# A pair of column blocks by seven products, and a plan laid a second time from its end

## What is computed

```python
h = rms_norm(x, norm_g) @ w_in
c_q, c_kv, k_pe, qkv_b, q_mem, gate = split_cols(h, EVEN_SPLITS)
...
o_b = moba_attention(q_b, k_b, v_b).transpose(0, 2, 1, 3).reshape(B, S, MOBA_HEADS * MOBA_DH)
o_m = memory_attention(q_mem, mem, mem_norm_g, w_mem_kv)
y = jnp.concatenate([o_a, o_b.astype(o_a.dtype), o_m.astype(o_a.dtype)], axis=-1) * jax.nn.silu(gate)
return x + (y @ w_out).astype(x.dtype)
```

## Time and profile before

| | us |
|---|---|
| median of 3 runs | 2955.57 (2954.85 to 2956.39) |
| the profiled execution, time | 2956.3 |
| the profiled execution, span of the core | 2954.5 |
| PE busy | 2936.6 |
| DVE busy | 2500.4 |
| ACT busy | 2233.4 |

### The profile page before, as it was taken

The page is one execution under the profiler, slowest core; times in us unless marked ns, Lnnn a source line. Parts: engine busy times, 40 slices in busy tenths (PEclk is TensorE's granted clock), DMA queues, the critical chain, the costliest instruction groups (busy, mean ns, idle before and its releaser), DMA issues.

```text
span 2954.5 us, 37919 instructions
## 1 busy us (share of the span) xinstructions
PE 2936.6 (99%) x13523; PEld 2453.0 (83%) x13523; DVE 2500.4 (85%) x3968; ACT 2233.4 (76%) x3815; POOL 10.5 (0%) x25
## 2 busy tenths in 40 slices
PE   8999999999999999999999999999999999999998
PEld 7888888878888888888888888888888888888887
DVE  6667679898887699999988888878999998888887
ACT  8788886966777668798985557776769899655684
POOL 0000000000000000000000000000000000000000
PEclk9999999999999999999999999999999999999999
DMA  9656555665556666556565665666665666566565
GB/s 331 192 168 184 173 195 178 210 187 180 180 176 201 193 208 195 174 173 192 178 190 185 207 207 192 214 201 188 192 202 175 188 178 186 188 202 208 175 203 178
DMA packets 305965, 570.52 MB, mean 193 GB/s; under 512 B 18432, under 2 KB 45216, under 8 KB 305392
## 3 DMA queue, kind: packets, MB, share of 16 engines
q1 hardware_dynamic: 301728, 557.65, 60.5%
q10 hardware_dynamic: 3040, 6.42, 0.6%
q0 software_dynamic: 1008, 4.02, 0.4%
HBM read 565.92 MB, written 2.10 MB: 192 GB/s over the span
## 4 chain that ended last, share of the span: by engine, by line
PE 97%; DVE 1%; ACT 1%; DMA 1%; issue 0%; DVEq 0%; SPq 0%; ACTq 0%
PE gp L152 86%; PE bk L152 10%; ACT G L167 1%; DVE wl L178 1%; DMA raw<-in_w_in 0%; ACT wh L167 0%; DVE nat L178 0%; DMA raw<-in_ev_w_mem_kv 0%; DVE merged L231 0%; PE bk L155 0%; DVE nat L184 0%; DVE merged L178 0%; DVE raw L178 0%; DVE merged L191 0%; ACT nat L167 0%
## 5 line engine op out<-in xcount | busy, mean ns | idle before, releaser
L167 ACT ACTIVATE wh<-raw 128x1024 fp32r<-128x1024 f32 (+3 forms) x1130 | 1141.9, 1024 | 570.2 <-PE gp L152 472.7
L178 DVE TENSOR_TENSOR wl<-raw,wh 128x1024 fp32r<-128x1024 f32 (+3 forms) x1130 | 1312.4, 1177 | 305.2 <-ACT wh L167 296.7
L152 PE MATMUL gp<-wh,Hh 128*128 128x512 f32 (+3 forms) x2133 | 826.9, 388 | 0.6 <-DVE wl L178 0.5
L152 PE MATMUL gp<-wl,Hh 128*128 128x512 f32 (+3 forms) x2133 | 819.3, 384 | 0.0
L152 PE MATMUL gp<-wh,Hl 128*128 128x512 f32 (+3 forms) x2069 | 794.4, 384 | 0.0
L152 PE MATMUL gp<-wh,Yh 128*128 128x512 f32 (+2 forms) x1774 | 689.8, 389 | 9.2 <-DVE wl L178 9.2
L152 PE MATMUL gp<-wl,Yh 128*128 128x512 f32 (+2 forms) x1774 | 684.8, 386 | 0.0
L152 PE MATMUL gp<-wh,Yl 128*128 128x512 f32 (+2 forms) x1710 | 659.9, 386 | 0.0
L152 PEld LDWEIGHTS gp<-wh,Hh 128*128 128x128 f32 x2133 | 400.7, 188 | 80.0 <-DVE wl L178 1.5
L152 PEld LDWEIGHTS gp<-wl,Hh 128*128 128x128 f32 x2133 | 400.8, 188 | 77.1
L152 PEld LDWEIGHTS gp<-wh,Hl 128*128 128x128 f32 x2069 | 388.6, 188 | 76.3
(11 more groups left out here) (188 smaller groups left out, 2216.4 us busy)
## 6 DMA issues: line engine op xcount, KB each, us to landing
raw<-in_w_in SPq DMA_DIRECT2D x544, 512.0 KB, 4.3
raw<-in_ev_w_in SPq DMA_DIRECT2D x104, 512.0 KB, 4.1
raw<-in_od_w_in SPq DMA_DIRECT2D x80, 512.0 KB, 4.0
raw<-in_w_out SPq DMA_DIRECT2D x64, 512.0 KB, 5.1
raw<-in_ev_w_out SPq DMA_DIRECT2D x40, 512.0 KB, 4.4
raw<-in_od_w_out SPq DMA_DIRECT2D x36, 512.0 KB, 4.5
raw<-in_w_b_out SPq DMA_DIRECT2D x32, 512.0 KB, 4.5
raw<-in_w_a_out SPq DMA_DIRECT2D x32, 512.0 KB, 4.9
```

The costliest lines, as they stand in the source:

```text
L152: return self.e.matmul(out, l, r, start=start, stop=stop)
L167: return self.e.activation(out, in_, func, **kw)
L178: return self.sketch(157 + size(a) * 1.042) if self.e is None else self.e.tensor_tensor(out, a, b, op)
```

## The change

It does two things. `hvg3_0`, the pair of v3 and gate3, joins `DUOS` with the order `VG2`, in which row block pairs 3 and 6 are starred and the other six go by plain products. And the plan is laid twice: first as before; then `latest` goes through the laid steps from the end of the plan to its start and finds for each step the latest begin that still keeps all that follows it; then `settle` lays everything again with that latest begin as the urgency, for all engines and all four layers. Some waits that named only the last piece of an operand now name all of its pieces (`pieces`), since the pieces may now be made in any order.

```diff
-DUOS = ('gate2', 'gate3', 'out3', 'out2', 'out0', 'hqk7_1')
+DUOS = ('gate2', 'gate3', 'out3', 'out2', 'out0', 'hqk7_1', 'hvg3_0')
...
-         ... "hqk7_1": QK7, "hvg7_1": VG7}
+         ... "hqk7_1": QK7, "hvg3_0": VG2, "hvg7_1": VG7}
...
+    def latest(self):
+
+        given, named, after = {}, {}, {}
...
+        for s in self.steps:
+            for a, when in needs(s):
+                if a is not s:
+                    when = 2000.0 + a.dma / 400.0 + a.late if a.dma else when
+                    after.setdefault(id(a), []).append((s, when + (self.LATE[s.engine] if a.engine != s.engine else 60.0)))
...
+        begin, taken = {}, {e: [] for e in ENGINES}
+        for s in sorted(self.steps, key=lambda s: -s.begin - s.took):
+            end = min([self.length] + [begin[id(b)] - lag + s.took for b, lag in after.get(id(s), ()) if id(b) in begin])
+            spans = taken[s.engine]
...
+            begin[id(s)] = last - s.took
+            spans.insert(i, (last - s.took, last))
+        return {(s.engine, s.name, s.args): begin[id(s)] for s in self.steps}
...
+    def pieces(self, kind, n):
+        return [(kind, n, i) for i in range(0, self.groups[n].blocks if kind == "y" else 16, 2)]
...
-            return [self.v_in.at(("mem", 0, 14))]
+            return [self.v_in.at(*self.pieces("mem", 0))]
...
         P.plan.settle(urgency(P, P.plan))
+        for _ in range(1):
+            begin = P.plan.latest()
+            P.plan.settle(lambda s, t: begin.get((s.engine, s.name, s.args), 0.0))
+        P.plan.close()
```

More of the change, by code:

```diff
@@ L49 @@
 ORDER = {**{f"gate{br}{n}{L}": w for L, of in ((2, GATES_OF_2), (3, GATES_OF_3)) for (br, n), w in zip(GATES, of)},
-         "ub0": UB0, "ub1": UB1, "out0": OUT0, "out1": OUT1, "out2": OUT2, "out3": OUT3, "end0": END0, "end1": END1, "end2": END2, "mem0": MEM0, "hvg2_0": VG2, "hqk2_0": QK2, "hqk7_1": QK7, "hvg7_1": VG7}
+         "ub0": UB0, "ub1": UB1, "out0": OUT0, "out1": OUT1, "out2": OUT2, "out3": OUT3, "end0": END0, "end1": END1, "end2": END2, "mem0": MEM0, "hvg2_0": VG2, "hqk2_0": QK2, "hqk7_1": QK7, "hvg3_0": VG2, "hvg7_1": VG7}
 SUMS = {k: tuple(sorted({int(w[1:]) for v in vs for w in v.split() if w[0] == "*"}))
@@ L282, in sketch, with needs @@
             programs[s.engine][s.name](*s.args)
-    def settle(self, urgency):
-        given = {}
+    def latest(self):
+        given, named, after = {}, {}, {}
+        for s in self.steps:
+            named[s.engine, s.name, s.args] = s
+            for signal, key, when in s.ups:
+                given[signal, key] = s, when
+        def needs(s):
+            for signal, key in s.waits:
+                yield given[signal, key]
+            for ring, name, _ in s.takes:
+                if name in ring.before:
+                    yield given[ring.before[name]]
+        for s in self.steps:
+            for a, when in needs(s):
+                if a is not s:
+                    when = 2000.0 + a.dma / 400.0 + a.late if a.dma else when
+                    after.setdefault(id(a), []).append((s, when + (self.LATE[s.engine] if a.engine != s.engine else 60.0)))
+            for b in s.behind:
+                a = named[s.engine, *b]
+                after.setdefault(id(a), []).append((s, a.took))
+        begin, taken = {}, {e: [] for e in ENGINES}
+        for s in sorted(self.steps, key=lambda s: -s.begin - s.took):
+            end = min([self.length] + [begin[id(b)] - lag + s.took for b, lag in after.get(id(s), ()) if id(b) in begin])
+            spans = taken[s.engine]
+            i = 0
+            while i < len(spans) and spans[i][0] <= end - s.took:
+                i += 1
+            last = min(end, spans[i][0]) if i < len(spans) else end
+            while i and last - s.took < spans[i - 1][1]:
+                i -= 1
+                last = spans[i][0]
+            begin[id(s)] = last - s.took
+            spans.insert(i, (last - s.took, last))
+        return {(s.engine, s.name, s.args): begin[id(s)] for s in self.steps}
+    def settle(self, urgency):
+        self.order, given = {}, {}
+        for r in self.rings:
+            r.which, r.before = {}, {}
+        for s in self.steps:
+            s.ready = 0.0
         for s in self.steps:
@@ L367, in settle, with close @@
             self.done += 1
-        count = {}
+        self.order = order
+        self.length = max(clock.values())
+    def close(self):
+        order, count = self.order, {}
         for e in ENGINES:
@@ L372, in settle @@
                     signal.value[key] = count[signal] = count.get(signal, 0) + (16 if s.dma else 1)
-            self.order[e] = [(s.name, s.args) for s in order[e]]
+            order[e] = [(s.name, s.args) for s in order[e]]
         self.open = False
-        self.length = max(clock.values())
 class Gemm:
@@ L889, in free_sums @@
         if L == 2:
-            return [self.v_in.at(("y", 9, 2), ("y", 6, 2))]
-        return [self.v_in.at(("y", 13, 2), *(("m", 0, i) for i in range(0, 16, 2)))]
+            return [self.v_in.at(*self.pieces("y", 9), *self.pieces("y", 6))]
+        return [self.v_in.at(*self.pieces("y", 13), *(("m", 0, i) for i in range(0, 16, 2)))]
     def both(self, L):
@@ L923, in room @@
         if gid == 0:
-            return [self.v_in.at(("x", 0, 14), ("ckv", 0, 0))]
+            return [self.v_in.at(*self.pieces("x", 0), ("ckv", 0, 0))]
         if gid == 1:
-            return [self.v_in.at(("mem", 0, 14))]
+            return [self.v_in.at(*self.pieces("mem", 0))]
         if gid == 6:
-            return [self.v_in.at(("mem", 1, 14))]
+            return [self.v_in.at(*self.pieces("mem", 1))]
         if old is None:
@@ L931, in room @@
         if all_of_it or not self.groups[old].carried:
-            got = [self.v_in.at(("y", old, self.groups[old].blocks - 2))]
+            got = [self.v_in.at(*self.pieces("y", old))]
         else:
@@ L953, in spare @@
         r = self.region[{("x", 2): 1, ("m", 0): 1, ("m", 1): 1}.get(of, 0)]
-        last = {("x", 1): ("y", 4, 2), ("x", 2): ("y", 8, 0), ("x", 3): ("y", 12, 2), ("m", 0): ("y", 13, 2),
-                ("m", 1): ("y", 17, 2)}[of]
+        last = {("x", 1): 4, ("x", 2): 8, ("x", 3): 12, ("m", 0): 13,
+                ("m", 1): 17}[of]
         a, b = ("kq" if of[0] == "m" else "kv", "qg")[c % 2]
-        return r[a].rearrange("p (t c) -> p t c", t=2), r[b], self.v_in.at(last)
+        return r[a].rearrange("p (t c) -> p t c", t=2), r[b], self.v_in.at(*self.pieces("y", last))
     def gathered(self, of, i):
@@ L1129, in clear_turn @@
         if gm.kind == "mk":
-            return [self.v_in.at(("y", 4, 2))] if gm.L else []
+            return [self.v_in.at(*self.pieces("y", 4))] if gm.L else []
         if gm.kind == "ckv":
@@ L1133, in clear_turn @@
         if gm.kind == "swkv":
-            return [self.v_in.at(("y", 3, 2))]
+            return [self.v_in.at(*self.pieces("y", 3))]
         if gm.kind == "ki":
-            return self.room(11 + 4 * (gm.L - 2), False) + [self.v_in.at(("y", 6, 2))]
+            return self.room(11 + 4 * (gm.L - 2), False) + [self.v_in.at(*self.pieces("y", 6))]
         if gm.kind == "ka":
@@ L1237, in load_mem2 @@
     def load_mem2():
-        e.wait_ge(*P.v_in.at(("y", 3, 2)))
+        e.wait_ge(*P.v_in.at(*P.pieces("y", 3)))
         e.dma_start(P.memT, P.ins["memT"]).then_inc(*P.s_mem2.up("mem", 16))
@@ L1298, in load_gfin @@
         g = (I["final_norm_g"], I["final_norm_w_2"])[f]
-        e.wait_ge(*P.v_in.at(*([("m", 1, i) for i in range(0, 16, 2)] if f else [("y", 9, 2)])))
+        e.wait_ge(*P.v_in.at(*([("m", 1, i) for i in range(0, 16, 2)] if f else [*P.pieces("y", 9)])))
         e.dma_start(P.gfin[f], g.unsqueeze(0).broadcast_to([128, 2048])).then_inc(*P.s_gfin[f].up("g", 16))
     def load_second():
-        e.wait_ge(*P.v_in.at(("y", 7, 2), ("y", 8, 0)))
+        e.wait_ge(*P.v_in.at(*P.pieces("y", 7), *P.pieces("y", 8)))
         e.dma_start(P.tab[:, :, :], I["c_tab2"]).then_inc(*P.s_tab2.up("t", 16))
@@ L1318, in load_cc @@
         else:
-            e.wait_ge(*P.v_in.at(("y", 1, 2)))
+            e.wait_ge(*P.v_in.at(*P.pieces("y", 1)))
         e.dma_start(P.cc[:, :], I["taps"][l]).then_inc(*P.s_cc.up(l, 16))
@@ L1323, in load_cc @@
         else:
-            e.wait_ge(*P.v_in.at(("y", 5, 2), ("y", 6, 2)))
+            e.wait_ge(*P.v_in.at(*P.pieces("y", 5), *P.pieces("y", 6)))
         e.dma_start(P.ones, I["c_ones"]).then_inc(*P.s_ones.up(l, 16))
@@ L1695, in evac @@
         if kind == "mv" and gm.L:
-            e.wait_ge(*P.v_in.at(("y", 4, 2)))
+            e.wait_ge(*P.v_in.at(*P.pieces("y", 4)))
         b = P.nat.buf(g)
@@ L1745, in evac @@
                         e.wait_ge(*w)
-                    e.wait_ge(*P.v_in.at(("y", 6, 2)))
+                    e.wait_ge(*P.v_in.at(*P.pieces("y", 6)))
                 e.activation(b[:, t, 0:128], p[:, 0:128], ACT.Copy, scale=sc)
@@ L2456, in move_latent @@
         e.wait_ge(*P.v_lflip.at(name))
```

(6 more changed lines are left out.)

## The result

The changed kernel takes 2960.16 us (median of 20 runs, 2958.94 to 2961.56), the kernel before 2955.98 in the same 20 rounds. The ratio is 1.0014, with a 95% interval of 1.0008 to 1.0020. It is inside my range (2951.6 to 2962.5) and inside the 0.2% that I had called "the same", but the interval leaves out 1: the change makes the kernel slower by a little, and I had forecast a little faster.

What follows compares the result with a forecast made beforehand. PE's own work was taken to bound the kernel. The span summed as 2954.5 - 1.36 + 0.3 - 0.85 + 1.0 = 2953.6 us; from the median of 2955.57, less 0.9, the forecast was 2954.7 us, range 2951.6 to 2962.5.

Steps and rivals of the forecast that it cites:

- What bounds the kernel: Whole kernel: PE's own work is nearly everything, at 0.227 us per matmul; its mid-kernel stalls cost only 1.70 us.
- the six matmuls: In v3 and gate3, two starred row block pairs take 21 matmuls instead of 24, saving PE 1.36 us.
- Banks and the values: Held banks delay group 3's scores and values; the memory group's 1.1 us margin before out0's `*8` shrinks, costing 0.3 us.
- ACT's overflow: In v3 and gate3, about 1 us of ACT's added work spills later; splits five fills ahead cover it, cost 0.
- Rival C: Banks, values and memory group stall PE 4 us before out0's `*8`, plus 1.0 elsewhere: 2958.4 us; chance 0.14.
- Small matmuls at no cost: Attention's small matmuls, spread singly between fills, cost PE nothing for switching; one head's scores take 0.66 us either way.
- The new order: On DVE and ACT, due times recover half the stalls, -0.85 us, and bring one new stall, +1.0 us.
- Rival B: Crowded stretches of the last two layers: splits lose their reserve, many short PE stalls, 2963 to 2971.9 us; chance 0.17.
- Rival D: Throughout PE: weight loads, not matmul spacing, are the limit, so time could shrink towards 2472 us; chance 0.01.
- Rival A: Both mid-kernel stalls go and out0 loses nothing: 2952.5 us, or 2952 with some of the end; chance 0.20.
- rival E: Second laying gives nearly the first order, only the pair counts: 2954.2 to 2955 us; inside the forecast's 0.46 chance.
- The chances: Whole kernel's time: faster by over 0.2% (5.9 us) 0.03, same 0.79, slower by more 0.18.

Runs made afterwards that it cites:

- e3_y3dve: Changed kernel with all four quarters of group 3's rows moved by DVE instead of two; 2953.32 us, 2953.25 us when run again.
- e6_y3only: Second laying without the pair, with all four quarters of group 3's rows moved by DVE; 2954.33 us, ratio 0.9994.
- e5_load: e2_plan with high parts of gate3's first four row block pairs made in eight pieces each on ACT; 2959.25 us, ratio 1.0011.
- e2_plan: Changed kernel without the pair hvg3_0, so the second laying alone; 2954.48 us, ratio 0.9995.
- e7_stars_first: Changed kernel with the pair's two seven-product row block pairs at the start of its order; 2957.83 us, ratio 1.0006.
- e4_stars_last: Changed kernel with the pair's two seven-product row block pairs at the end of its order; 2959.80 us, ratio 1.0013.
- e10_one6: Changed kernel with only row block pair 6 starred and 3 plain; 2954.98 us, ratio 0.9996.
- e8_late8: Changed kernel with row block pairs 5b and 7b of out0 run before the starred 8; 2955.20 us, ratio 0.9998.
- e9_orders: e3_y3dve with other orders of row block pairs in the new pair and in out0; 2954.50 us, ratio 0.9994.

## Why the prediction was wrong

**What bounds the kernel, and the six matmuls: right.** The spacing stayed 0.227 in all kernels, and the stalls tell nearly all of the time. Where nothing new stalls, the pair is worth 1.0 us by medians (`e3_y3dve` against `e6_y3only`) beside the 1.36 worked out.

**"Banks and the values": the step that failed.** I had found the place, the margin of 1.1 us before `*8`, and what presses on it: held banks, late values, ACT's backlog and PE's earlier arrival. I then took 0.3 us out of bounds of 0 and 4. It measured 5.1 us of stall and 1.5 us of slow clock. Two reasons that I gave for the low end were wrong. ACT's 18 us of idle time between lie in small pieces, where ACT waits for PE's buffers; an idle sum isn't room for a chain. And the second laying was to rank this chain by its due time, but it laid two low parts of weights ahead of it, and the wait for `Hl` is 1.1 us longer with it than without. The upper bound was also too low: it counted added work, and not that group 3's moves would fall among the memory group's and bring splits between them. The product with the values was to come some 10 us later; it came 18 and 21 us later. The scores were nearer: I had 352, and they run from 346.3 to 353.1.

**"I cost this at nothing", ACT's overflow: failed.** Five fills of lead cover the splits. They don't cover the moves that stand in the same queue: in `e5_load` 2.6 us more on ACT end in a stall of 3.7 us at `*8`.

**Rival C** named this mechanism and gave 2958.4; it got 0.14 of the chance. With 1.5 us for the clock it would have been 2959.9, beside the measured 2960.16. That it comes so near is in part luck: its 4 us before `*8` were 1.1 too few, and its +1.0 - 0.85 for the new order stood where the stall of 1.02 us near 2815 us went. I left the clock out although the first matmuls of the kernel before run slowly as well.

**Small matmuls at no cost: right.** One head's scores alone, between large matmuls, take 0.66 us after the change too (from 352.86 to 353.97, less two of 0.227).

**The new order:** the sum had -0.85 + 1.0; `e2_plan` has -1.6 by medians. One of the two stalls went (1.02 us). By PE's starts three small ones of 0.3 us went too (near 1177, 1821 and 2167 us), and two of 0.3 and 0.4 came (near 211 and 2674). **Rival B** (no reserve) didn't come about: in the stretches of the earlier trace rows there is no new wait. **Rival D** didn't either. **Rival A** wanted both stalls gone, and **rival E** nothing changed by the laying; one stall went.

**The chances.** I let "within 0.2%" hold most of the chance and asked little of the sign inside it. Twenty rounds told a difference of 0.14% from none.

## What to carry to other kernels

When one engine is busy all the time, look for the smallest margin between a chain of the others and that engine, and ask of every added instruction whether it stands in a queue ahead of that chain; a sum of idle time says nothing on it. A saving and the work that pays for it should be weighed by that margin: here one starred row block pair, with the banks taken after the scores, fitted and two didn't, and moving 3.4 us of another group's moves to another engine brought the gain back. Ask of every shared bank who waits for it while it is held, and whose queue that user will then be in. Cost a stall of PE with what follows it, since the clock may fall.

## What the runs showed of the hardware

After some pauses of PE the clock fell, and after others it didn't. Near 454 us of `e7_stars_first` PE was idle for 1.8 us and worked on at full speed for five matmuls, and then eight ran with starts 0.427 us apart, at a granted clock of 0.62 from 455.5 to 460 us. After a wait of 3.5 us alone (`e5_load`) it was 0.57 from 456 to 460; after 4.45 us (`e4_stars_last`) 0.50 from 366 to 370. Waits of 0.86 us, of 0.6 us in `e10_one6`, of 1.0 us in `e8_late8` (near 491 us), of 1.1 us in `e9_orders` (near 321) and of 1.2 us in `e7_stars_first` itself (near 327) had no slow matmuls behind them. Each slow matmul costs 0.2 us more. "TensorE: Matmul & The Clock Gate" of the Trainium skill, section "HAM oscillation — how this bites in real kernels", describes such a fall after idle gaps of TensorE; the traces agree that it falls, and show it also after the 1.8 us named here.
